# Sixteen unused floats in front of part one's operands: a shift of its tensors by 64 bytes

## The reference

```python
h = _rms_norm(x, in_norm_g[l])
y = h @ w_in[l] + b_in[l]
# mLSTM (4 heads), HGRN2 (4 heads), sliding-window attention (8 heads) on columns of y
x = x + jnp.concatenate([m_out, h_out, s_out], axis=-1) @ w_out[l]
u = _rms_norm(x, mlp_norm_g[l]) @ w_up[l]
x = x + jnp.square(jax.nn.relu(u)) @ w_down[l]
gate = jax.nn.sigmoid((_rms_norm(x, ple_norm_g[l]) @ w_ple_gate[l]).astype(jnp.float32))
e = _rms_norm(p[l] @ w_ple_proj[l], ple_post_norm_g[l]).astype(jnp.float32)
x = x + (gate * e).astype(x.dtype)
```

## The kernel before

| tensor | address before | in 128 | in 256 | address of the change | in 128 | in 256 |
|---|---|---|---|---|---|---|
| `high_panels` | 50336 | 32 | 160 | 50336 | 32 | 160 |
| `low_panels` | 74912 | 32 | 160 | 74912 | 32 | 160 |
| `h1_high` | 132576 | 96 | 224 | 132640 | 32 | 32 |
| `mlp1_h_high`, `ple_h_high` | 144864 | 96 | 224 | 144928 | 32 | 32 |
| `arena1` | 165344 | 96 | 224 | 165408 | 32 | 32 |
| `mlp1_hid_high` | 177632 | 96 | 224 | 177696 | 32 | 32 |
| `h2_high`, `mlp2_h_high` | 116128 | 32 | 160 | 116128 | 32 | 160 |
| `mlp2_hid_high` | 148896 | 32 | 160 | 148896 | 32 | 160 |

## Time and profile before

### The profile page before, as it was taken

One profiled execution on the slowest core, in us unless ns is written; L12 is line 12 of the kernel. 1 busy time (PEld: TensorE's weight loads), 2 busy tenths in 40 slices (PEclk: granted clock), 3 DMA queues, 4 the chain that ended last, 5 costly groups with the idle time before them and its releaser, 6 DMA issues. The chain is left out here.

```text
span 2966.0 us, 37027 instructions
## 1 busy us (share of the span) xinstructions
PE 2815.3 (95%) x14756; PEld 2340.2 (79%) x14756; DVE 1615.2 (54%) x2705; ACT 1128.1 (38%) x1712; POOL 193.0 (7%) x192
## 2 busy tenths in 40 slices
PE   6999899999899899999989999899998999899998
PEld 5877788888788677888878878788887887788887
DVE  5755566655765648555576434543544534454443
ACT  6445322223554433322354444432323344332232
POOL 1310100002121110000120000100000000100001
PEclk9987999999899699999999999999998999999999
DMA  4210154343221014444422111223222210122322
GB/s 158 72 43 29 54 187 179 144 169 114 102 79 58 15 61 161 155 164 149 170 84 90 57 34 40 83 85 110 93 76 103 72 42 31 57 100 79 114 82 68
DMA packets 42978, 278.80 MB, mean 94 GB/s; under 512 B 6072, under 2 KB 6456, under 8 KB 11704
## 3 DMA queue, kind: packets, MB, share of 16 engines
q1 hardware_dynamic: 42808, 276.44, 26.4%
HBM read 274.33 MB, written 2.10 MB: 93 GB/s over the span
## 5 line engine op out<-in xcount | busy, mean ns | idle before, releaser
L306 DVE TENSOR_TENSOR low_panels<-raw_panels,high_panels 128x2048 fp32r<-128x2048 f32 (+3 forms) x218 | 469.6, 2154 | 337.9 <-ACT high_panels L293 337.8
L293 ACT ACTIVATE high_panels<-raw_panels 128x2048 fp32r<-128x2048 f32 (+3 forms) x218 | 392.6, 1802 | 460.4 <-PE bank L1549 149.4
L424 PE MATMUL bank<-mlp_h_high,high_panels 128*128 128x512 f32 x1152 | 451.8, 392 | 0.0
L424 PE MATMUL bank<-mlp_h_high,low_panels 128*128 128x512 f32 x1152 | 450.6, 391 | 0.0
L424 PE MATMUL bank<-mlp_h_low,high_panels 128*128 128x512 f32 x1152 | 449.2, 390 | 0.0
L424 PEld LDWEIGHTS bank<-mlp_h_high,low_panels 128*128 128x128 f32 x1152 | 216.5, 188 | 45.7
L424 PEld LDWEIGHTS bank<-mlp_h_low,high_panels 128*128 128x128 f32 x1152 | 216.4, 188 | 45.6
L424 PEld LDWEIGHTS bank<-mlp_h_high,high_panels 128*128 128x128 f32 x1152 | 216.5, 188 | 44.4
L449 PE MATMUL bank<-high_panels,h_high 128*128 128x256 f32 x704 | 206.5, 293 | 0.5 <-ACT values_and_ones L2061 0.5
L424 PE MATMUL bank<-h_high,high_panels 128*128 128x512 f32 x496 | 203.5, 410 | 0.2
L1549 PE MATMUL bank<-mlp_hid_high,high_panels 128*128 128x512 f32 x512 | 203.4, 397 | 0.0
(11 more groups left out here) (346 smaller groups left out, 5111.4 us busy)
## 6 DMA issues: line engine op xcount, KB each, us to landing
raw_panels<-in_w SPq DMA_DIRECT2D x236, 1024.0 KB, 4.8
raw_panels<-in_w SPq DMA_DIRECT2D x16, 384.0 KB, 3.1
raw_panels<-in_w SPq DMA_DIRECT2D x4, 960.0 KB, 4.6
raw_panels<-in_w SPq DMA_DIRECT2D x4, 768.0 KB, 4.1
row<-in_row SPq DMA_DIRECT2D x2, 1220.0 KB, 6.1
x<-in_xT SPq DMA_DIRECT2D x2, 1024.0 KB, 6.0
raw_panels<-in_w SPq DMA_DIRECT2D x4, 512.0 KB, 3.4
mix<-in_rope SPq DMA_DIRECT2D x2, 1024.0 KB, 6.1
```

Source lines behind the costliest of these rows:

```text
L293: self.nc.scalar.activation(self.g.high[:, j % SPLIT, 0:raw.shape[1]], raw, ACT.Copy).then_inc(self.high_ready, 1)
L306: self.nc.vector.tensor_tensor(self.g.low[:, j % SPLIT, 0:w], raw, self.g.high[:, j % SPLIT, 0:w].bitcast(F32), ALU.subtract).then_inc(sel ...
L424: ins = nc.tensor.matmul(bank[:, :], w[a][:, k, c0:c0 + P], rhs[b][:, k0 + k, :], start=first and k == 0 and j == 0, stop=last and k == kt ...
```

## The change

One tensor of 16 floats a partition is opened in `part_one` behind `row_of_ones`. Nothing writes or reads it. All that part one opens after it (the dense operands of `layer_one`, `mlp_one` and `embedding_gate`, `arena1`, and the small buffers of these stages) starts 64 bytes further on. Shared tensors, panels and all of part two keep their addresses, and every engine's instructions stay the same, in the same order, with the same waits; line numbers behind L474 grow by one.

```diff
--- before.py
+++ after.py
@@ -472,6 +472,7 @@
         small = sb("small1", [P, 320])
         ones = sb("row_of_ones", [P, S])
         g.row_of_ones = ones[:, :]
+        sb("space_one", [P, 16])
 
         with nc.Block() as block:
             e = NormSignals(s, "start")
```

## The result

| | before | change |
|---|---|---|
| median, 6 executions each | 2967.08 us (2960.52 to 2970.28) | 2986.04 us (2977.21 to 2990.98) |
| ratio | | 1.0064, 95% interval 1.0046 to 1.0081 |
| profiled execution | 2967.89 us, span 2966.0 | 2986.29 us, span 2984.3 |

The change costs 0.64%, 18.9 us. The forecast of 2963.9 us and its range are missed, and on the other side.

A forecast was written before the change was run, and what follows sets the result against it. TensorE's matmul spacing was taken to bound the kernel: -10.2 us feature, +8.1 token, -1.5 hidden in `layer_one`, in sum -3.6 against the profiled 2967.89; with the median 0.36 lower, 2963.9 us. The range was 2957.0 to 2971.5 us.

The forecast's parts named there:

- What bounds the kernel: Feed-forward stages: time is matmul count times distance between starts; TensorE 95% busy, pace changes paid or gained in full.
- VectorE, ScalarE and the arena: Whole kernel: the new place costs these engines and matmuls reading the arena nothing; term zero.
- If the period is 128, part one becomes like part two in both forms: Part one's feature and token matmuls: a 128-byte block decides their pace, giving 7 ns less a triple, 6 ns more a token matmul.
- the feature term: Part one's feature matmuls: 1456 triples each give back 7 ns, 10.2 us gained; bounds nothing and 10.2 us.
- its main risk: Part one's operands: the period may be 256 or more, or operand distance may count; no row has the new place.
- the reading in which it didn't matter: Part one takes part two's pace in both forms, whole kernel 2960 to 2966 us; chance 0.53.
- The token term: `layer_one`: 1344 token matmuls each cost 6 ns more, 8.1 us lost; bounds nothing and 8.1 us.
- What `layer_one` hides: `layer_one`: shrinking TensorE waits absorb a quarter of the net +6.2 us, 1.5 us; bounds nothing and 4.6 us.
- small risk: Whole kernel: the granted clock's low stretches may come to lie otherwise, making the prediction wrong by a little; no term.
- Rival 1: Whole kernel: nothing moves, paces differ between parts for something other than low address bits; 2967.5 us, chance 0.2.
- Rival 2: Part one: feature gain of 10.2 us without the token loss; 2957.5 us, chance 0.17.
- Rival 3: Part one: token loss without feature gain, 2973.6 us, or a feature pace worse still; chance 0.1 together.

The follow-up runs named there:

- arena_64: Kernel before with `arena1` alone moved up 64 bytes, dense operands left in place; 2965.11 us, ratio 1.0006.
- all64: Kernel before with `x`, panels and all activations moved up 64 bytes together, every distance kept; 2961.25 us in one execution.
- a256_b192: Kernel before with part one's operands moved up 256 bytes and part two's 192; 2989.16 us in one execution.
- layer_one_64: Kernel before with only the operands of `layer_one` and its arena moved up 64 bytes; 2975.23 us, ratio 1.0029.
- feed_64: Kernel before with only the operands of `mlp_one` and `embedding_gate` moved up 64 bytes; 2977.13 us, ratio 1.0036.
- feed_192: Kernel before with `mlp_one` and `embedding_gate` operands moved up 192 bytes to distance 0, `layer_one` left at 64; 2964.14 us, ratio 0.9993.
- feed_192_two_64: Kernel before with `mlp_one` and `embedding_gate` operands at distance 0 and `layer_two` moved to distance 64; 2962.52 us, ratio 0.9986.
- act_low_192: Kernel before with only the low activations of `mlp_two` at distance 192, panels unmoved; 2971.16 us in one execution, against 2964.26 beside it.
- a192: Kernel before with part one's operands moved up 192 bytes, to distance 0; 2970.21 us against 2965.79, ratio 1.0011.
- a32_b32: Kernel before with part one's and part two's operands each moved up 32 bytes, to distances 96 and 32; 3005.94 us in one execution.
- a128_b64: Kernel before with part one's operands moved up 128 bytes (distance 192), part two's 64 (distance 64); 2983.63 us in one execution.
- a160_b160: Kernel before with part one's and part two's operands each moved up 160 bytes, to distances 224 and 160; 3005.33 us in one execution.
- the swap: Another name for a128_b64: kernel before with part one's operands up 128 bytes and part two's up 64; 2983.63 us in one execution.

## Why the prediction was wrong, step by step

**What bounds the kernel: right.** `mlp_one` grew by 4.2 and 3.7 us, and nothing in it but the matmuls' pace got slower. 1024 triples at 10 ns are 10.2 us; 2.4 us less at the lower clock give back about 1.2 of them, and 7.9 were measured. The difference of 1.1 us is not accounted for. VectorE, ScalarE and the arena were put at zero, and the rows and `arena_64` show zero.

**The step that failed** is the sentence "If the period is 128, part one becomes like part two in both forms", on which the feature term of -10.2 us stands. The period is 256 bytes, and it is the distance between the two operands that has it, not the place of each (`all64`, `a256_b192`). The prediction named this as its main risk and knew that the new distance, 128, had no row. It still gave 0.53 to the reading in which it didn't matter, because that was the simplest reading of two points. Two points fit any period. In place of 7 ns gained, 10 ns are lost: 1456 x 10 ns = +14.6 us.

**The token term** was right in sign and too large: +4.3 ns each instead of 6, 1344 x 4.3 ns = +5.8 us instead of 8.1. Part of that was a matter of reading: the 6 ns were a difference of two medians of durations, while the distance of two starts, which is what TensorE pays, differs by 5.4 ns between the two places in the kernel before (114.3 and 119.7). The sign was right by the wrong reason, for every distance other than 64 is worse in this form.

**What `layer_one` hides.** Its two stages carry 5.8 us of the token form and 272 x 10 ns = 2.7 us of the feature form, 8.5 us, and grew by 5.7 at the same time at the lower clock: 2.8 hidden. The forecast took a quarter of its net 6.2, at most three quarters; it is a third of the 8.5 here, and at equal clock `layer_one_64` shows 4.1 of 8.5 paid, which hides half. The waits of the three arena lines shrank by 3.9 us, which is the mechanism that was named. How much is hidden stays uncertain: in the profiles of five other kernels whose `layer_one` operands lie at before's distance (`all64`, `feed_64`, `feed_192`, `feed_192_two_64`, `act_low_192`) the two stages took 638.2 to 646.6 us together, where before has 643.3.

**The clock was not priced.** The prediction named it as a small risk and gave it no term. The change ran at a mean of 0.9603, the kernel before at 0.9634; by the line above, about 5.9 us go with that, and 14.1 with the pace. (Their sum is 20.0, the mean of the six executions less the line's 2965.6; the 18.9 are a difference of medians.) By pace alone the terms are 14.6 + 5.8 us, less 2.8 to 4.4 hidden in `layer_one`, 16.0 to 17.6: two to three us more than the 14.1, and that rest is open. `layer_one_64` has the same low mean and `feed_64` and `arena_64` don't, so it goes with the place of `h1_high` and `h1_low`. That this place causes it rests on five and more executions of each kernel, and why it should is open: `a192` has it too, with other paces, while `a32_b32`, `a128_b64` and `a160_b160`, which move the two tensors as well, read 0.963, 0.965 and 0.965 in one execution each. The stage table doesn't show it where one would look: in the profiled pair 8.8 us more are at the lower level, worth up to half of it, 4.4 us, but none of them in `layer_one`. They lie in `embedding_gate`, 6.4 us, and in part two, 5.0, less 2.4 in `mlp_one`; and `feed_64`, whose mean is not lower, has 6.0 us more in `embedding_gate` too.

**The rivals.** Rival 1 is refuted by the swap. Rival 2, the gain without the loss, did not come: neither half holds. Rival 3 came, in the version of its last sentence but one, "A feature pace that is worse still at the new distance ends on this side too", which was given part of 0.1 and no price, and which the range left out. The forecast's arithmetic was tested by `a192`, where the premise does hold: -3.6 us were forecast, -2.8 were measured at equal clock, and nothing in the raw median. Even there, the feature gain was real and mostly paid back in `layer_one`.

**The Trainium skill's rule** that the streaming operand and the weight load have read ports of their own, and that the spacing of matmuls goes by their columns ("TensorE: Matmul & The Clock Gate", "Step-by-step: what each phase is for" and "Back-to-back issue gap"), was weighed against two rows and set aside. The measurement decides more sharply now: with the same columns, eight distances give 680 to 703 ns for a triple. Whatever the ports are, the pace of this stream depends on where its two operands lie to each other.

## What to carry to other kernels

Where TensorE is saturated with short-spaced matmuls, look at the distance between the start addresses of the two operands within 256 bytes, and mind its sign: here the worst placing that was run cost 40 us (3006 against 2966, one execution), and a pad of a few floats sets it. The kernel before was placed well already; the best of the others that was timed more than once gained 0.14%. Before believing a period from two points, list which value of every candidate variable (place, distance, block) the change will have, and if none of the rows has it, price both signs. Judge such an edit by the durations of one form at full clock, and only then by the total, since 0.001 more of granted clock goes with 1.9 us less in this kernel.

## What the runs showed of the hardware that was not expected

- The pace of a 128x512 float32r product depends on the distance between its operands modulo 256 bytes: 226.7 ns at 0, 229 at 64, 232 to 234 elsewhere, in steps of 32 bytes. A shift of both by 64 bytes, or of the activation by 256, left it as it was.
- The 128x256 form with the activation as weights has another best distance, 64 (activation less panel; 114 to 116 ns), and its worst, 119.7 to 119.8, at 0 and 160, while 0 is the best of the other form.
- With one of the two panel tensors at distance 192 a triple costs 13 ns more, with one of the two activations there 7, with all of it there 20; which reads meet is open.
- With no instruction changed, the mean granted clock of an execution lay between 0.957 and 0.967, and moving two tensors of `layer_one` by 64 bytes went with a mean that was 0.003 lower; the cause is open.
